# Spreading the last level of a block inverse by parity of the head, and moving inverse steps ahead of attention steps in four queues

## What is computed

```python
# group A, per head (4 heads, dk = dv = 128) and chunk of 64 tokens
a = jnp.where(strict, jnp.einsum('bhncd,bhnsd->bhncs', kb, k) * decay, 0.0)
lower = a + jnp.eye(CHUNK, dtype=f32)
u = lax.linalg.triangular_solve(lower, v * beta[..., None], ...)
w = lax.linalg.triangular_solve(lower, kb * jnp.exp(gc)[..., None], ...)
# then a scan over the chunks with a state of 128 x 128 per head

# group B (8 query heads, 2 key heads of 64, window of 128 tokens)
m = jnp.maximum(jnp.max(s, axis=-1, keepdims=True), sink)
p = jnp.exp(s - m)
p = p / (jnp.sum(p, axis=-1, keepdims=True) + jnp.exp(sink - m))
```

## Time and profile before

| what | us |
|---|---|
| median of 3 runs | 2383.08 (2381.32 to 2383.19) |
| the profiled execution, its own time | 2381.3 |
| its span, from the first to the last instruction | 2379.7 |
| PE busy / PEld busy | 2337.7 / 1925.2 |
| DVE busy / ACT busy / POOL busy | 1427.3 / 955.7 / 162.6 |

### The profile page before, as it was taken

One profiled execution on the slowest core, in us unless ns is written; L12 is line 12 of the kernel. 1 busy time (PEld: TensorE's weight loads), 2 busy tenths in 40 slices (PEclk: granted clock), 3 DMA queues, 4 the chain that ended last, 5 costly groups with the idle time before them and its releaser, 6 DMA issues.

```text
span 2379.7 us, 36988 instructions
## 1 busy us (share of the span) xinstructions
PE 2337.7 (98%) x12942; PEld 1925.2 (81%) x12942; DVE 1427.3 (60%) x2089; ACT 955.7 (40%) x1714; POOL 162.6 (7%) x183
## 2 busy tenths in 40 slices
PE   6999999999999999999999999999999999999998
PEld 4888888888888888888888888888888887888886
DVE  7786652454778665255568866425457875642644
ACT  5566321223466532122346643212234764321232
POOL 0131000000012000000001200000000130000000
PEclk9999999999999999999999999999999999999999
DMA  4222322233321223224332132322433213322241
GB/s 159 98 72 72 97 97 97 97 132 115 126 82 61 90 95 100 97 89 142 118 121 73 53 107 89 98 97 97 141 120 120 71 46 106 98 97 97 97 146 66
DMA packets 64007, 236.66 MB, mean 99 GB/s; under 512 B 7568, under 2 KB 7696, under 8 KB 62720
## 3 DMA queue, kind: packets, MB, share of 16 engines
q1 hardware_dynamic: 55728, 201.98, 25.7%
q0 software_dynamic: 8144, 32.94, 3.9%
HBM read 226.47 MB, written 8.42 MB: 99 GB/s over the span
## 4 chain that ended last, share of the span: by engine, by line
PE 85%; DVE 9%; issue 3%; ACT 2%; DMA 0%; DVEq 0%; ACTq 0%; POOL 0%; POOLq 0%
PE ps L1468 84%; DVE w_l L886 1%; PE ps L1626 1%; DVE nq L1013 1%; DVE state L1284 1%; DVE nq_l L1018 0%; DVE h_l L1402 0%; DVE qkvz L1075 0%; DVE acc L900 0%; DVE qkvz L1079 0%; DVE ti L1298 0%; DVE sm L1050 0%; DVE qk L1067 0%; DVE at L1048 0%; DVE d L1042 0%
## 5 line engine op out<-in xcount | busy, mean ns | idle before, releaser
L1468 PE MATMUL ps<-h_h,w_h 128*128 128x512 f32 x2004 | 792.4, 395 | 8.7 <-DVE h_l L911 4.6
L1468 PE MATMUL ps<-h_l,w_h 128*128 128x512 f32 x2004 | 782.2, 390 | 0.0
L1468 PE MATMUL ps<-h_h,w_l 128*128 128x512 f32 x1972 | 767.8, 389 | 0.0
L497 ACT CAST w_h<-stage 128x1024 fp32r<-128x1024 f32 x381 | 398.2, 1045 | 559.5 <-PE ps L1468 559.5
L886 DVE TENSOR_TENSOR w_l<-stage,w_h 128x1024 fp32r<-128x1024 f32 x381 | 466.7, 1225 | 251.6 <-ACT w_h L497 238.1
L1468 PEld LDWEIGHTS ps<-h_h,w_h 128*128 128x128 f32 x2004 | 376.9, 188 | 107.4 <-DVE h_l L911 10.8
L1468 PEld LDWEIGHTS ps<-h_l,w_h 128*128 128x128 f32 x2004 | 377.5, 188 | 76.7 <-issue 1.9
L1468 PEld LDWEIGHTS ps<-h_h,w_l 128*128 128x128 f32 x1972 | 370.1, 188 | 77.8
L1468 PE MATMUL ps<-ff_h,w_h 128*128 128x512 f32 x1036 | 404.6, 391 | 0.0
L1468 PE MATMUL ps<-ff_h,w_l 128*128 128x512 f32 x1036 | 403.1, 389 | 0.0
L1468 PE MATMUL ps<-ff_l,w_h 128*128 128x512 f32 x1036 | 403.1, 389 | 0.0
(11 more groups left out here) (196 smaller groups left out, 1824.8 us busy)
## 6 DMA issues: line engine op xcount, KB each, us to landing
stage<-w SPq DMA_DIRECT2D x385, 512.0 KB, 3.3
x_next<-x POOLq DMA_DIRECT2D x20, 512.0 KB, 6.0
out<-xs POOLq DMA_DIRECT2D x32, 256.0 KB, 2.3
rowb<-row_copy POOLq DMA_DIRECT2D x4, 1024.0 KB, 4.9
xs<-x POOLq DMA_DIRECT2D x8, 512.0 KB, 4.8
xs<-x POOLq DMA_DIRECT2D x4, 1024.0 KB, 5.4
bia<-bias POOLq DMA_DIRECT2D x1, 1024.0 KB, 6.6
cst<-con POOLq DMA_DIRECT2D x2, 192.0 KB, 3.5
```

What stands on the lines that cost most here:

```text
L497: act.copy(w_h[:, b, 0:k], stage[:, s, 0:k]).then_inc(w_hi.sem, 1)
L1468: return pe.matmul(o, a, b, start=start, stop=stop)
```

## The change

Four things change, in the stage in question only.

1. **Spreading.** The second `turn` becomes `turn_apart`: rows by the chunk, columns by the parity of the head, so that four consecutive products use four quarters. `corner_masked` puts even heads to the left and odd heads to the right (two quarters). `corner_update` takes even heads from the upper rows and odd heads from the lower rows (two quarters). All three go by pairs of tiles.
2. **Copies.** ACT's `flip` of level 1 (4 copies 64 x 256 into `xi`) becomes `keep_low` (2 copies 128 x 256 into `x_blk`). ACT's `corner` (4 copies 64 x 512) becomes 8 copies 64 x 256, four for each pair. DVE's last mask (4 copies 64 x 256) becomes `corner_mask`, 2 copies 128 x 256.
3. **POOL.** It gets 2 copies of 64 partitions x 512 from `x_blk` to `xi`, between `probabilities(2)` and `probabilities(3)`. `values(0)` waits for them (`low_put`).
4. **Order.** On PE, `turn_apart` and `corner_masked` come ahead of `sc(3)`, and `corner_update` comes ahead of `sc(4)` and `pt(2)`. On DVE, the level 1 masks come ahead of `maximum(1)`, `extend(1)` ahead of `scores(2)`, `corner_mask` ahead of `softmax(2)`, and `softmax(2)` and `softmax(3)` stand ahead of the next `scores`. On ACT, `keep_low` comes ahead of `exps(2)`.

The core of the diff:

```diff
+        def from_rows(pair, e, turned):
+            return ps[:, lev(pair[e]), 0 if turned else 256:][:, 0:256].rearrange("p (x c) -> p x c", c=HD)
...
+                    if n == 3:
+                        pool.wait_ge(x_ready.sem, x_ready.after(g, 2 * TILES))
+                        pool.wait_ge(A["p_ready"].sem, A["p_ready"].after(g, n))
+                        pool.nop(nofuse=True)
+                        for odd in range(2):
+                            nc.gpsimd.tensor_copy(xi[64:P, :, :, 64:P].rearrange("p t (j two) c -> p two t j c", two=2)[:, 1 - odd],
+                                                  x_blk[chunk(1 - odd), :, 0:2]).then_inc(low_put.sem, 1)
...
+                def keep_low(pair):
+                    act.wait_ge(p_x.sem, p_x.after(g, TILES + pair[1] + 1))
+                    act.copy(x_blk[:, pair[0]:pair[0] + 2, 0:2].rearrange("p t j c -> p t (j c)"),
+                             from_rows(pair, 1, True).rearrange("p (t j) c -> p t (j c)", t=2)).then_inc(x_ready.sem, 2)
+                def corner(pair):
...
+                    for turned in (True, False):
+                        cols = slice(0, 64) if turned else slice(64, P)
+                        act.copy(of_parity(pair, 0, cols), from_rows(pair, 0, turned)[0:64])
+                    act.copy(of_parity(pair, 1, slice(0, 64)), from_rows(pair, 0, True)[64:P])
+                    act.copy(of_parity(pair, 1, slice(64, P)), from_rows(pair, 1, False)[0:64]).then_inc(x_ready.sem, 2)
...
+                def turn_apart(pair):
...
+                    for n, t in enumerate(pair):
+                        for j in range(2):
+                            for e in range(2):
+                                for odd in range(2):
+                                    last = mm(from_rows(pair, e, True)[chunk(odd), 2 * n + j], t_blk[chunk(e), slot(t), 2 * j + odd],
+                                              cst[chunk(e), K_ID, chunk(e)])
+                        last.then_inc(p_x.sem, 1)
+                def corner_masked(pair):
+                    for n, t in enumerate(pair):
+                        for h in range(HEADS):
+                            last = mm(from_rows(pair, 0, False)[chunk(h % 2), 2 * n + h // 2], at_[0:64, t, h, 64:P], t_blk[0:64, slot(t), h])
+                        last.then_inc(p_y.sem, 1)
+                def corner_update(pair):
...
+                        for h in range(HEADS):
+                            r, j = chunk(h % 2), h // 2
+                            last = mm(from_rows(pair, h % 2, False)[0:64, 2 * n + j], dl[r, t, HD * j:HD * j + HD], x_blk[r, t, j])
...
                 for pair in PAIRED:
                     update(1, pair)
-                sc(3)
                 ov(0)
                 for pair in PAIRED:
-                    turn(1, pair)
+                    turn_apart(pair)
+                for pair in PAIRED:
+                    corner_masked(pair)
+                sc(3)
                 pt(1)
-                for t in range(TILES):
-                    corner_masked(t)
                 ov(1)
+                for pair in PAIRED:
+                    corner_update(pair)
                 sc(4)
                 pt(2)
-                for t in range(TILES):
-                    corner_update(t)
                 key_states(0)
```

More of the change, by code:

```diff
@@ L773, in _ @@
                 for t in range(TILES):
-                    flip(0, t)
+                    flip(t)
                 exps(1)
                 pt_copy(0)
+                for pair in PAIRED:
+                    keep_low(pair)
                 exps(2)
-                for t in range(TILES):
-                    flip(1, t)
                 pt_copy(1)
@@ L782, in _ @@
                 att_out(0)
-                for t in range(2):
-                    corner(t)
+                corner(PAIRED[0])
                 pt_copy(2)
-                for t in range(2, 4):
-                    corner(t)
+                corner(PAIRED[1])
                 exps(4)
@@ L1322, in _ @@
                 softmax(0)
+                for t in range(TILES):
+                    mask(1, t)
                 maximum(1)
                 for t in range(TILES):
-                    mask(1, t)
+                    extend(1, t)
                 scores(2)
@@ L1328, in _ @@
                 softmax(1)
-                for t in range(TILES):
-                    extend(1, t)
+                for pair in PAIRED:
+                    corner_mask(pair)
                 softmax(2)
@@ L1333, in _ @@
                 maximum(3)
-                mask(2, 0)
-                mask(2, 1)
                 softmax(3)
-                for t in range(2, 4):
-                    mask(2, t)
                 scores(4)
@@ L1677, in update, with turn @@
                                     last.then_inc(p_u.sem, 1)
-                def turn(l, pair):
-                    pe.wait_ge(t_ready.sem, t_ready.after(g, l * TILES + pair[1] + 1))
+                def turn(pair):
+                    pe.wait_ge(t_ready.sem, t_ready.after(g, pair[1] + 1))
                     pe.nop(nofuse=True)
@@ L1686, in turn @@
                                 r = chunk(e)
-                                o = across(e, t) if l == 0 else r
-                                last = mm(ps[o, lev(t), HD * h:HD * h + HD], t_blk[r, slot(t), h], cst[r, K_ID, r])
+                                last = mm(ps[across(e, t), lev(t), HD * h:HD * h + HD], t_blk[r, slot(t), h], cst[r, K_ID, r])
                                 if h == HEADS - 1 and e:
                                     last.then_inc(p_x.sem, 1)
-                def corner_masked(t):
-                    pe.wait_ge(x_ready.sem, x_ready.after(g, (LEVELS - 2) * TILES + t + 1))
+                def turn_apart(pair):
+                    pe.wait_ge(t_ready.sem, t_ready.after(g, TILES + pair[1] + 1))
@@ L1695, in corner_masked @@
                     pe.nop(nofuse=True)
-                    four(ps[64:P, lev(t), 0:256].rearrange("p (h c) -> p h c", h=HEADS),
-                         lambda o, h: mm(o, at_[0:64, t, h, 64:P], t_blk[0:64, slot(t), h]), p_y)
-                def corner_update(t):
-                    pe.wait_ge(y_ready.sem, y_ready.after(g, (LEVELS - 1) * TILES + t + 1))
-                    pe.nop(nofuse=True)
-                    four(ps[0:64, lev(t), 256:512].rearrange("p (h c) -> p h c", h=HEADS),
-                         lambda o, h: mm(o, dl[64:P, t, 64 * h:64 * h + 64], xi[64:P, t, h, 64:P]), p_u)
+                    for n, t in enumerate(pair):
[5 more added lines that the diff above has]
+                        last.then_inc(p_x.sem, 1)
@@ new lines, in corner_masked @@
+                def corner_masked(pair):
[4 more added lines that the diff above has]
+                def corner_update(pair):
+                    pe.wait_ge(y_ready.sem, y_ready.after(g, (LEVELS - 1) * TILES + pair[1] + 1))
+                    pe.wait_ge(x_ready.sem, x_ready.after(g, TILES + pair[1] + 1))
+                    pe.nop(nofuse=True)
+                    for n, t in enumerate(pair):
+                        for h in range(HEADS):
+                            r, j = chunk(h % 2), h // 2
+                            last = mm(from_rows(pair, h % 2, False)[0:64, 2 * n + j], dl[r, t, HD * j:HD * j + HD], x_blk[r, t, j])
+                        last.then_inc(p_u.sem, 1)
@@ L1719, in values @@
                     pe.wait_ge(x_ready.sem, x_ready.after(g, LEVELS * TILES))
+                    if t == 0:
+                        pe.wait_ge(low_put.sem, low_put.after(g, 2))
                     if t >= 2:
@@ L1749, in _ @@
                 for pair in PAIRED:
-                    turn(0, pair)
+                    turn(pair)
                 for pair in PAIRED:
```

44 lines of the change are left out of this document (22 added, 22 removed).

## The result

| what | us |
|---|---|
| before, median of 10 runs | 2382.45 (2381.32 to 2383.19) |
| after, median of 10 runs | 2388.24 (2386.52 to 2389.88) |
| after : before | 1.0024, 95% interval 1.0016 to 1.0032 |
| the profiled execution after, its own time / span | 2389.88 / 2388.3 |
| PE busy before / after | 2337.7 / 2334.9 |

The change makes the kernel 5.8 us slower. Forecast were 2388.9 us and +5.8. The profiled execution after is the slowest of its ten, so its span shows 8.6 us more, not 5.8. Of these 8.6, 1.4 us lie ahead of the first masked(0) (167.75 against 166.35), where the program is the same. The ten executions differ in their mean granted clock: the three at 0.995 took 2389.74 to 2389.88 us, the five at 0.997 or 0.998 took 2386.52 to 2388.90, 5.1 above before on average.

The account below looks back on a forecast made before the run. PE bounds the kernel before; afterwards ACT's and DVE's chain delays key_states(0) by 1.55 + 4.3 = 5.8 us over four groups, so 2381.3 becomes 2387.1, plus 1.8 to the median: 2388.9, range 2383 to 2392 (0.8).

Parts of the forecast that it names:

- the chain of ACT and DVE: From masked(0) to key_states(0), later exps, copies and softmax steps make key_states(0) 1.55 us later in the first group.
- The POOL copy: First new copy takes 1.25 us and holds DVE's step 3 product with the sink until it ends, losing 1.00.
- the missing wait ahead of key_states(0): Sign: key_states(0) waits about 3 us a group for ACT's copy into xi; under 2 us means the forecast is wrong.
- the short sink product: Sign: DVE's step 3 product with the sink takes 1.1 to 1.2 us, not 0.16; if short, the forecast is wrong.
- some 11: Sign: PE's busy time over the whole kernel falls by some 11 us while the span grows.
- theory O: Said ahead of e3: maximum(1) ahead of the masks brings the chain to key_states(0) 0.6 to 0.8 us earlier, about 2385.7.
- PE stands idle for about 3.1 ahead of key_states(0): PE's own work ends at 183.3, so the 3.3 us saved a group are lost there and in two smaller waits.
- A similar gap further on would fall on sc(3) and be covered too: A second "issue" gap on PE, like the 0.56 us one in update(1), would cost nothing.
- near 1.1: Sign: corner_masked and corner_update on PE each take near 1.1 us, with two quarters at 30 ns a pass.
- Nothing more is late: Behind key_states(0), pt(3), values(0) and scores(4) have their inputs in time, so no further loss is added.
- the rivals: Sink product ahead of POOL copy, 2384.9 (0.2); copy 1.7 us or more, 2390.7 to 2392.4 (0.12); PE stays the bound.
- PE stays the bound: Rival: the change gives the 4 x 3.3 = 13 us it removes from PE, 2370 us; chance 0.05, half of it 0.07.

Follow-up runs that it names:

- e9: Changed kernel with PE's new order kept, but the order of before on DVE and ACT: 2388.66 us, ratio 1.0032.
- e5: Changed kernel with corner_update on PE moved between pt(1) and ov(1): 2388.44 us, ratio 1.0026.
- e7: Changed kernel plus six products on PE ahead of ov(1), filling its wait without changing results: 2386.87 us, ratio 1.0019.
- e3: Changed kernel with maximum(1) on DVE again ahead of the level 1 masks: 2385.28 us, ratio 1.0013.
- e2: Kernel before, without spreading or POOL copies, with PE, DVE and ACT in the new order: 2388.87 us, ratio 1.0026.
- e6: Changed kernel with the two POOL copies behind probabilities(3) instead of ahead of it: 2388.73 us, ratio 1.0025.
- e4: Changed kernel with exps(2) on ACT again ahead of the two keep_low copies: 2388.16 us, ratio 1.0025.
- e12: e8 with DVE's att_out(0) moved ahead of scores(4) and maximum(4): 2373.93 us, ratio 0.9964.
- e8: e1 with both corner_masks ahead of softmax(3) on DVE and corner_update ahead of sc(4) and pt(2) on PE: 2373.72 us, ratio 0.9961.
- e10: e8 with corner_masked on PE ahead of pt(1) instead of between pt(1) and ov(1): 2382.49 us, ratio 1.0000.
- e11: Changed kernel with 32 empty instructions on PE ahead of masked(0), which left no record: 2389.15 us, ratio 1.0027.
- e1: Changed kernel with all queues back in the order of before, keeping the spreading, its copies and the POOL copies: 2378.07 us, ratio 0.9982.

## Why the prediction was right, and where its steps were not

The sign and the number held. Of the mechanism, the chain of ACT and DVE held up to exps(2); what came behind it was in part another. That +5.8 was forecast and +5.8 measured is luck: the POOL copy was overrated by about as much as PE's losses, which the sum hadn't, added. Two of the prediction's own signs of being wrong came true, the missing wait ahead of key_states(0) (it allowed no less than 2 us) and the short sink product (0.34); and PE's busy time fell by 2.8 us, not by some 11, much of what it saved going at the low clock: in e9, where the clock stayed up, it is 14.36 in the first group's stretch, against 17.04 before and 15.66 here.

**The chain of ACT and DVE: right.** exps(1) starts 7.61 behind masked(0) (forecast 7.62), exps(2) 12.10 (12.02), ov(0) 9.96 (9.92). e5 and e7 give PE back what it lost behind pt(1), in two ways, and both leave 78.2 us to key_states(0), +3.6 over before, with PE waiting for ACT in all eight groups: a floor set by ACT, in part of the groups with sc(3) ahead of it. e3 gives the price of maximum(1), 0.8 a group, as theory O had it. e2 shows that with this order the spreading is worth nothing.

**The POOL copy: mis-sized.** It took 0.67, not 1.25. The blocking of the product with the sink is real, but costs 0.18 and not 1.00 (0.34 in three groups of e5), and in e6, where it is gone, the time is the same. exps(3) came 16.15 behind masked(0) and not 16.74: 0.82 less for the copy, and 0.24 more because the product with the sink started at 15.78 and not 15.54, mostly since scores(3) waited for sc(3).

**"PE stands idle for about 3.1 ahead of key_states(0)": failed.** In the changed kernel PE and ACT arrive together: corner(0)'s last copy ends at 187.40, and key_states(0) follows pt(2) at 187.48 without a wait. The forecast had PE there 16.95 behind masked(0); it was 19.73, 2.8 later. It had lost 2.5 of this in three places that I had left out or sized wrongly, and the rest in sc(4) and pt(2), which ran at the low clock too:
- "A similar gap further on would fall on sc(3) and be covered too": it came, 0.97 us in the first group (1.26 in the last). It was not covered: scores(3) waited for sc(3), though in the first group only 0.17 longer than for softmax(2), and pt(1), pt_copy(1) and ov(1) behind it were late by all of it. With exps(2) earlier (e4), scores(3) waits 0.82.
- pt(1) and ov(1) are neighbours in the new order, and I had taken ov(1) to follow pt_copy(1) without asking what PE does meanwhile: 0.8 us idle.
- corner_update "near 1.1": 1.87, at a granted clock of 0.56. Without PE's wait ahead of ov(1) it stays at 1.00 (e5, e7).

**"Nothing more is late": failed.** sc(4) came late, so scores(4), and DVE's att_out(0) behind it, for which ov(2) waits: 0.54 to 0.58 a group. e12 shows the dependence, in e8's order: with att_out(0) ahead of scores(4) the stretch is 2.71 again.

**Which part of the order:** I laid the loss to DVE and ACT. e9 shows that PE's order alone makes exps(3) late: it starts 14.7 to 15.5 behind masked(0) with the old order on DVE and ACT, since sc(3) comes late. e10 shows the same for pt(1) (14.4 to 14.7). Both limits lie close together in the changed kernel, and undoing one alone (e4, e5, e6) brought nothing in the median; e3 brought 3.0. Of the rivals none came true; "PE stays the bound" was nearer than its 0.05, but as a PE that had lost its gain.

## What to carry to other kernels

When a bound engine gets faster, put the freed time where another engine's answer is awaited: the same spreading gave -4.5 us in the old order, -8.8 with the corner's products ahead of two independent steps, nothing where in addition a product and the step that waits for its copy were made neighbours (e10), and +5.8 with the whole new order. Price a merged order by what stands between each request and its use on every engine, and look for a second limit just below the first before undoing one thing at a time. Small products made denser can bring stalls without a releaser, and short idle times can bring the low clock; the sum of durations shows neither.

## What the hardware showed that I had not expected

**Stalls marked "issue".** That PE waits for instructions in them is argued from their places; no run shows the fetch itself, and e11, which was to move them, didn't (its empty instructions left no record). Between two of them (the one ahead of ov(2), which waits for att_out(0), is none) there are 125 or 126 passes, each a weight load and a matmul, whatever lies between: update(1)'s 42nd pass to the first of sc(3) in the changed kernel (22 + 8 + 64 + 32 = 126), to the 16th of corner_masked in e10 (22 + 16 + 8 + 64 + 16 = 126), to the 11th in e1 (125). In the first group after the change an instruction queue moved four packets in 22 us, 0.07 MB in all:

```profile
q8 instruction: 4, 0.07, 1.2%
```

The stall was 0.97 us in the first group after the change, where turn_apart and corner_masked ran back to back at 15 and 29 ns a pass, 0.57 (0.84 to 0.86 in the other groups) within corner_masked in e10, 0.3 in e1 with pt(1) between them, and there was none where PE ran slower (e2; the second group of e11).

The Trainium skill ("Runtime: NRT & Kernel Launch", Instruction fetch mechanics) says that instructions are fetched in blocks of 16 KiB, which are 256 instructions. The 250 to 252 counted, with the waits and register instructions between them, agree. It also says that the cost of crossing a block is "mostly hidden"; for dense quarter products the measurement decides, and the stall was 0.97 us, if it is this crossing.

**The clock.** With the stall as PE's last idle time the granted clock stayed at 1.00 (e5, e7). With the wait ahead of ov(1) but no stall ahead of sc(3) it stayed at 1.00 as well (e2). With both it fell to 0.56 over ov(1) and corner_update in all groups after the change and in all of e4, in two of e10, in one of e3 and in none of e9, at a price of 0.8 us in corner_update alone. In e6 and e11, which have the changed kernel's order on PE, it fell there in five of eight groups; in the other three it was low earlier, over turn_apart, and sc(3) came without a stall. So the two idle times together don't decide it. What sets the kernels apart is that ov(0), just before them, waits for ACT (0.19 to 0.74 us) after the change and in e4, and doesn't in e3, e9 and e10; why the groups of e3 and e10 differ among themselves isn't shown.
